# Hybrid trunk layer on one core: order of the first loads, small tables on the scalar engine's queue, first group's matmuls interleaved with the transposes of x

## The reference

```python
for l in range(DEPTH):                                  # DEPTH = 1, x is 1 x 256 x 2048 float32
    h = rmsnorm(x, pre_norm_g[l])
    proj = jnp.einsum('bsd,dn->bsn', h, w_in[l])        # 2048 x 18776
    (da_q, da_k, da_v, da_z, ml_qk, ml_v, ml_if, ml_o, ml_z,
     dsa_q, dsa_kv, idx_q, idx_k, idx_w, dsa_z, gates) = jnp.split(proj, split_points, axis=-1)
    y_a = diff_attention(...) * silu(da_z)
    y_b = mlstm(...) * silu(ml_z)
    y_c = dsa_attention(...) * silu(dsa_z)
    g = sigmoid(gates)
    mixed = sum over the three branches of g_b * (y_b @ w_branch[l, b])
    x = x + rmsnorm(mixed @ w_out[l], post_norm_g[l])
```

## Time and profile before

| | us |
|---|---|
| median of three runs | 1133.67 |
| span of the profiled execution, first to last instruction | 1131.5 |
| PE busy | 1110.0 (98%) |
| DVE busy | 657.7 (58%) |
| ACT busy | 549.5 (49%) |
| weights and x read from HBM | 202.57 MB, 181 GB/s over the span |

### The profile page before, as it was taken

The page is one execution under the profiler, slowest core; times in us unless marked ns, Lnnn a source line. Parts: engine busy times, 40 slices in busy tenths (PEclk is TensorE's granted clock), DMA queues, the critical chain, the costliest instruction groups (busy, mean ns, idle before and its releaser), DMA issues.

```text
span 1131.5 us, 15625 instructions
## 1 busy us (share of the span) xinstructions
PE 1110.0 (98%) x5143; PEld 915.0 (81%) x5143; DVE 657.7 (58%) x910; ACT 549.5 (49%) x736; POOL 70.8 (6%) x122
## 2 busy tenths in 40 slices
PE   7999999999999999999999999999999999999995
PEld 6788888888878888888887778888888888888884
DVE  4744444666566676665766566665556645556454
ACT  6644444555454554544546444454444544445442
POOL 1000000100100011120210000000000000000001
PEclk9999999999999999999999999999999999999998
DMA  8666666566556546666556556655555476676551
GB/s 245 223 190 192 197 188 197 173 170 183 167 169 175 167 140 184 192 180 184 169 168 192 164 157 191 205 167 163 166 163 160 129 222 191 197 238 229 196 195 75
DMA packets 112399, 205.09 MB, mean 181 GB/s; under 512 B 11064, under 2 KB 15728, under 8 KB 111984
## 3 DMA queue, kind: packets, MB, share of 16 engines
q1 hardware_dynamic: 112368, 204.70, 60.1%
HBM read 202.57 MB, written 2.10 MB: 181 GB/s over the span
## 4 chain that ended last, share of the span: by engine, by line
PE 95%; SPq 2%; DVE 1%; ACT 1%; issue 0%; DMA 0%; DVEq 0%; ACTq 0%
PE stream L1233 30%; PE stream L1235 30%; PE stream L1234 29%; SPq L367 1%; PE mixer L1469 1%; DVE area L1216 1%; DVE wlo L822 0%; PE mixer L1496 0%; PE mixer L1485 0%; PE mixer L1328 0%; PE mixer L1303 0%; PE mixer L1404 0%; PE mixer L1462 0%; PE mixer L1429 0%; PE mixer L1314 0%
## 5 line engine op out<-in xcount | busy, mean ns | idle before, releaser
L822 DVE TENSOR_TENSOR wlo<-raw,whi 128x1024 fp32r<-128x1024 f32 (+1 forms) x378 | 460.9, 1222 | 430.5 <-ACT whi L559 428.5
L559 ACT ACTIVATE whi<-raw 128x1024 fp32r<-128x1024 f32 (+1 forms) x378 | 397.7, 1054 | 553.6 <-PE stream L1235 537.9
L1233 PE MATMUL stream<-whi,xhi 128*128 128x512 f32 (+1 forms) x1312 | 518.6, 395 | 2.8 <-DVE wlo L822 2.4
L1235 PE MATMUL stream<-whi,xlo 128*128 128x512 f32 (+1 forms) x1312 | 510.1, 389 | 0.0
L1234 PE MATMUL stream<-wlo,xhi 128*128 128x512 f32 (+1 forms) x1312 | 509.0, 388 | 0.0
L1233 PEld LDWEIGHTS stream<-whi,xhi 128*128 128x128 f32 x1312 | 246.8, 188 | 56.6 <-issue 5.8
L1235 PEld LDWEIGHTS stream<-whi,xlo 128*128 128x128 f32 x1312 | 246.6, 188 | 51.6
L1234 PEld LDWEIGHTS stream<-wlo,xhi 128*128 128x128 f32 x1312 | 247.1, 188 | 48.1
L1233 PE MATMUL stream<-whi,yhi 128*128 128x512 f32 x192 | 77.1, 401 | 0.0
L1235 PE MATMUL stream<-whi,ylo 128*128 128x512 f32 x192 | 75.0, 391 | 0.0
L1234 PE MATMUL stream<-wlo,yhi 128*128 128x512 f32 x192 | 74.8, 390 | 0.0
(11 more groups left out here) (244 smaller groups left out, 567.9 us busy)
## 6 DMA issues: line engine op xcount, KB each, us to landing
raw<-in_w_in SPq DMA_DIRECT2D x288, 512.0 KB, 3.7
raw<-in_w_branch SPq DMA_DIRECT2D x48, 512.0 KB, 4.5
raw<-in_w_out SPq DMA_DIRECT2D x32, 512.0 KB, 3.7
mixed<-in_x SPq DMA_DIRECT2D x4, 512.0 KB, 6.0
raw<-in_w_in SPq DMA_DIRECT2D x8, 256.0 KB, 3.9
area<-in_x SPq DMA_DIRECT2D x2, 1024.0 KB, 9.2
out<-area SPq DMA_DIRECT2D x8, 256.0 KB, 2.3
raw<-in_dsa_w_uv SPq DMA_DIRECT2D x4, 256.0 KB, 3.0
```

What stands on the lines that cost most here:

```text
L559: nc.scalar.activation(whi[:, slot, :, 0:width], raw[:, slot, :, 0:width], ACT.Copy).then_inc(whi_ready, 1)
L822: nc.vector.tensor_tensor(wlo[:, slot, :, 0:width], raw[:, slot, :, 0:width], whi[:, slot, :, 0:width].bitcast(F32), ALU.subtract).then_in ...
L1233: nc.tensor.matmul(to, left_hi[:, kt, tokens], high, start=first, stop=False)
L1235: last = nc.tensor.matmul(to, left_lo[:, kt, tokens], high, start=False, stop=final)
```

## The change

SP: the three DMAs into `rows` leave SP's queue and are issued by ACT as its first instructions. x1 follows x0 directly, and then the order is small unit 0, x2, small unit 1, x3, small unit 2, small units 3 to 7, and last the six constants. Before, the constants stood ahead of unit 4. The loads of group PA follow as before, now behind the constants.

PE: after banks 0 to 3 of x it multiplies unit 0, transposes banks 4 and 5, multiplies unit 1, transposes banks 6 and 7, and then multiplies units 2 to 7.

ACT and DVE: the early units are handled one at a time, unit 0 after bank 1, unit 1 after bank 3, unit 2 after bank 5, unit 3 after bank 7. ACT's `square_x(1)` moves from behind the rounding of unit 7 to behind that of unit 5, and the rounding and the split of A0 move ahead of the square root and of the reciprocal.

```diff
@@ -97,7 +97,7 @@
                     turns, units, groups)
 
 
-EARLY_UNITS = {5: (0,), 7: (1, 2, 3)}
+EARLY_UNITS = {1: (0,), 3: (1,), 5: (2,), 7: (3,)}
 PS = Part(0, 0, 1, FULL_UNITS, 1)
 PA = PS.next(4, 2 * FULL_UNITS, 2)
 PB = PA.next(4, 2 * FULL_UNITS, 2)
@@ -371,21 +371,14 @@
             for n in range(X_LOADS):
                 part_of_x = slice(n * D_MODEL // X_LOADS, (n + 1) * D_MODEL // X_LOADS)
                 sp.dma_start(x_sb[:, :, part_of_x], x_d[:, :, part_of_x]).then_inc(x_landed[n], 16)
-                if n == 0:
-                    sp.dma_start(rows[40:56, :], pre_norm_g[0].rearrange("(b d) -> b d", d=P)).then_inc(rows_landed, 16)
-                    sp.dma_start(rows[0:32, :], ml_conv_w[0].rearrange("j (b d) -> (j b) d", d=P)
-                                 ).then_inc(rows_landed, 16)
-                    sp.dma_start(rows[32:40, :], ml_conv_b[0].rearrange("(b d) -> b d", d=P)).then_inc(rows_landed, 16)
-                if n >= 2:
-                    load_small(n - 2)
-            load_small(2)
-            load_small(3)
+                if n >= 1:
+                    load_small(n - 1)
+            for u in range(X_LOADS - 1, FULL_UNITS):
+                load_small(u)
             for to, of in ((lam_in[:, :, :].rearrange("p a b -> p (a b)"), da_lambda[0].rearrange("a b -> (a b)")),
                            (da_g[:, :], da_norm_g[0]), (ml_g[:, :], ml_norm_g[0]), (kv_g[:, :], dsa_kv_norm_g[0]),
                            (ik_g[:, :], dsa_ik_norm_g[0]), (gate_b[:, :], ml_gate_b[0].rearrange("a b -> (a b)"))):
                 sp.dma_start(to, of.partition_broadcast(P)).then_inc(consts_landed, 16)
-            for u in range(RING, FULL_UNITS):
-                load_small(u)
 
             with sp.Fori(0, PA.turns) as i:
                 for g in range(2):
@@ -566,6 +559,9 @@
                     nc.scalar.activation(to[t], stream[bank_pair][t][:, 0:width], ACT.Copy, scale=rstdx[:, t:t + 1]
                                          ).then_inc(banks_free, 1)
 
+            act.dma_start(rows[40:56, :], pre_norm_g[0].rearrange("(b d) -> b d", d=P)).then_inc(rows_landed, 16)
+            act.dma_start(rows[0:32, :], ml_conv_w[0].rearrange("j (b d) -> (j b) d", d=P)).then_inc(rows_landed, 16)
+            act.dma_start(rows[32:40, :], ml_conv_b[0].rearrange("(b d) -> b d", d=P)).then_inc(rows_landed, 16)
             act.wait_ge(cols_turned, 1)
             nc.scalar.activation(cols[:, :], M[0][:, 0:56], ACT.Copy).then_inc(cols_ready, 1)
             act.wait_ge(cols_ready, 1)
@@ -582,13 +578,14 @@
 
 
             square_x(0)
-            for u in range(FULL_UNITS // 2):
+            for u in range(FULL_UNITS // 2 + 1):
                 round_unit(PS, 0, u)
-            square_x(1)
+                if u == 1:
+                    square_x(1)
             act.wait_ge(msx_ready, 1)
             nc.scalar.activation(rstdx, rstdx, ACT.Sqrt).then_inc(stdx_ready, 1)
 
-            for u in range(FULL_UNITS // 2, FULL_UNITS):
+            for u in range(FULL_UNITS // 2 + 1, FULL_UNITS):
                 round_unit(PS, 0, u)
             act.wait_ge(rstdx_ready, 2)
             take_group(PS, 0, FULL_UNITS, 0, [small[:, t, :] for t in range(TILES)], SMALL)
@@ -849,12 +846,13 @@
                 split_unit(PS, 0, u)
             dve.wait_ge(ssx_ready, 2)
             nc.vector.tensor_scalar(rstdx, ssx, 1.0 / D_MODEL, EPS, ALU.mult, ALU.add).then_inc(msx_ready, 1)
+            split_unit(PS, 0, FULL_UNITS // 2)
             dve.wait_ge(stdx_ready, 1)
             nc.vector.reciprocal(rstdx, rstdx).then_inc(rstdx_ready, 1)
             dve.wait_ge(rstdx_ready, 1)
             nc.vector.tensor_scalar(half_rstdx, rstdx, 0.5, None, ALU.mult).then_inc(rstdx_ready, 1)
 
-            for u in range(FULL_UNITS // 2, FULL_UNITS):
+            for u in range(FULL_UNITS // 2 + 1, FULL_UNITS):
                 split_unit(PS, 0, u)
 
             dve.wait_ge(consts_landed, 6 * 16)
@@ -1256,11 +1254,14 @@
                                                    x_sb[:, t, kt * P:(kt + 1) * P], ident[:, :])
                 last.then_inc(x_turned, 1)
 
-            for b in range(8):
+            for b in range(4):
                 turn_x(b)
 
             pe.wait_ge(xlo_ready, 4)
             for u in range(FULL_UNITS):
+                if u in (1, 2):
+                    turn_x(2 * u + 2)
+                    turn_x(2 * u + 3)
                 pe.wait_ge(xlo_ready, UNIT_KT * (u + 1))
                 multiply(PS, 0, u, u, FULL_UNITS, 0, xhi, xlo, SMALL)
```

## The result

The changed kernel takes 1138.09 us in the median of four runs (1136.27 to 1139.65), the kernel before 1133.27 us in the same session (1132.83 to 1134.2). The ratio is 1.0044, with a 95% interval of 1.0032 to 1.0055: slower by 3.6 to 6.2 us, where the forecast was +3.2 us.

The account below looks back on a forecast made before the run. PE bounds the kernel, so only A4's start counts, set by `take_group`: 21.0 + 1.52 + 2.88 + 4.6 + 1.04 + 1.41 + 3.0 + 0.97 = 36.4 against 33.17, +3.2 us, 1136.9 us; range 1133.5 to 1138.8.

Parts of the forecast that it names:

- x's start: PE's start on x: set by x0 landing at 5.8 us (4.9 to 6.5), with the tables there by about 4.9.
- Interleaving: PE's early units and banks: 1.9 us a unit, 1.97 per two banks; ACT done with unit 3 at 20.0 us.
- SP's queue: SP from unit 3's split at 21.0 us: three issues 1.52, six constants 2.88; A0's load issued at 25.4.
- Flight of A0: A0's load from issue to landing: 4.6 us, bounds 3.7 and 5.7; it lands at 30.0 us.
- Three roundings and take_group: ACT behind the root: 3.0 us for three roundings, 0.97 for `take_group`, which ends at 36.4 us.
- take_group to A4: Small steps on DVE and ACT from `take_group`'s end to A4 on PE: unchanged 9.80 us, A4 at 46.2.
- rival 1: ACT never waits for A0, whose load gets out or lands in time: +0.2 us, 1133.9 us; chance 0.12.
- rival 2: PE is the bound up to A4, never waiting: A4 starts at 40.2, -2.8 us, 1130.9 us; chance 0.05.
- Rival 4: x3 lands late and holds PE's transposes: 1 us beyond the hidden part gives 1137.9 us; chance 0.02.
- Rival 3: PE's clock falls in the longer stall before A4, which runs at half speed: another 2.8 us, 1139.7; chance 0.04.

Follow-up runs that it names:

- e1: The changed kernel with SP issuing the six constants ahead of small unit 4 again: 1133.75 us, ratio 1.0001.
- e7: The kernel before plus 17 transposes of the identity on PE ahead of x, result unread: 1133.81 us, ratio 1.0002.
- e5: The changed kernel with the six constants issued by POOL instead of SP, after the fourth split: 1136.43 us, ratio 1.0030.
- e10: The changed kernel with the constants ahead of small unit 4 and ACT's and DVE's old order behind unit 3: 1135.52 us, ratio 1.0011.
- e6: The changed kernel with the three table DMAs back on SP and 17 transposes of the identity on PE ahead of x: 1139.70 us, ratio 1.0061.
- e9: The kernel before with the change's loads, but constants ahead of small unit 4, and `square_x(1)` directly behind `square_x(0)`: 1132.26 us, ratio 0.9992.
- e2: The changed kernel with the three table DMAs back on SP behind x0: 1139.41 us, ratio 1.0050.
- e3: The kernel before with only the change's loads (SP's new order, tables on ACT); PE, ACT and DVE keep their order: 1136.36 us, ratio 1.0024.
- e8: The kernel before with interleaving, the new x and small-unit load order, tables on SP, constants on POOL behind bank 5, 17 added transposes: 1135.01 us, ratio 1.0020.
- e4: The kernel before with only the new order on PE, ACT and DVE; SP's order and the tables as before: 1136.91 us, ratio 1.0029.

## Why the prediction was right, and where its size was off

The sign, the place and the chain were right: A0's load went out behind the constants at 25.27 (forecast 25.4), ACT stood still in front of it with root and `take_group` queued behind, A4 started by `take_group`'s chain, and nothing changed from there on. Run e1 shows it by undoing that one thing. The measured 1138.09 us lies in the range, near its upper end. By the steps:

| step | forecast | measured |
|---|---|---|
| PE begins on x | 5.8 | 7.14 |
| unit 3 rounded (T3) | 20.0 | 19.4 |
| unit 3 split | 21.0 | 20.6 |
| A0's load issued | 25.4 | 25.27 |
| A0 at ACT | 30.0 | 30.96 |
| `take_group` ends | 36.4 | 38.06 |
| A4 starts on PE | 46.2 | 47.51 |

- **x's start.** x0 did not set it. It landed 4.3 us after its issue, at 5.1; the tables did, at 6.8. I had let them land "by about 4.9 us", from their flight on SP's queue, where only x0's load was ahead of them, while I charged the company in flight to x0. The step failed by 1.3 us.
- **Interleaving.** That error was more than made good by a second one. I timed the transposes at 1.97 us for two banks from the earlier trace rows, twice. Behind unit 0 they took about 0.8 us, as the next matmul follows 0.79 us after them (13.89 to 14.68). The old figure was that of a PE at 1.2 GHz: run e7 turns the same banks in 1.1 us once PE has worked before them. T3 came out 0.6 us early, by luck: two errors of opposite sign.
- **SP's queue.** From unit 3's split to A0's issue were 4.67 us instead of 4.40. With the split 0.4 us early, the issue at 25.27 looks more exact than the working was.
- **Flight of A0.** This is the mis-sized term: 5.7 us, my upper bound, where I took 4.6. The row I took was of a load that went out when its slot came free, with the next 1.2 us behind it. Here four loads went out within 2 us, behind 0.5 MB of constants. Run e5 puts 6.95 us on the same load with the constants beside it and e1 3.6 us without, as does e10 with the loads crowded. I had this cost as a bound and not as a cause.
- **Three roundings and take_group.** The forecast was 3.0 us from A1 to `take_group`, without waits; it took 3.55, since A1 to A3 flew 7.6 to 8.9 us and ACT waited for two of them. A0's rounding, the table load and the root took 2.58 instead of 2.45.
- **take_group to A4.** 9.45 instead of 9.80 us. The time outside the profiled span was 1.8 us (1136.27 less 1134.5), where 2.2 was added.

The rivals: rival 1 (ACT never waits) and rival 2 (PE as the bound) fell, with a wait of 4.98 us and an A4 4.5 us later. Rival 4 fell as well: PE did not wait for x2 or x3. Rival 3 was half right. I gave it 0.04 with the argument that PE had idled 5.4 us at the start and still ran at 1.00. The clock did fall, not at A4 but within A0, in front of which PE had waited 2.38 us:

```profile
32.00:34.00 2.00, 0.67 (x2) 0.53 (x3) 1.56 (x3) 1.96 (x4) 0.00 (x0) 0.94 0.88 336
34.00:36.00 2.00, 2.00 (x6) 1.61 (x5) 1.30 (x2) 1.66 (x2) 0.00 (x0) 0.50 0.75 219
36.00:38.00 2.00, 2.00 (x7) 1.54 (x7) 1.93 (x2) 1.87 (x3) 0.00 (x0) 0.71 0.64 156
```

Matmuls of 512 columns came every 0.43 us there. It cost nothing by itself: A0 to A3 ended later, and PE's wait before A4 was 1.38 us instead of the 2.7 forecast. The argument was wrong at its root, see below. The Trainium skill's rule, "TensorE: Matmul & The Clock Gate", section "Why this matters for your kernels", that an idle gap between bursts brings 1.2 GHz back, agrees in kind with this stretch; I had set it aside on the strength of a column that could not speak against it. But not every such gap did: in e5 and e6 PE waited 2.56 us before A4, and the windows behind show 1.00. The row of e5:

```profile
46.12 0.50 PE L1232 MATMUL stream<-whi,xhi 128*128 128x512 f32 x1 [2.56 <-DVE wlo L820]
```

What stays open: whether e9's 0.08% is real, and how much of the spread of the changed kernel is the clock of its start. The mean granted clock of its four executions (0.995, 0.993, 0.995 and 0.993 for spans of 1134.5, 1137.9, 1136.4 and 1136.2 us) does not put them in order.

## What to carry to other kernels

When DMAs are moved in a queue that also waits for slots, look for the first big load behind their new place and ask two things: when it is issued, and what flies beside it; small broadcast loads cost more in the second way (2.5 us in run e5) than in the first (1.4). An order that interleaves compute with loads moves the time at which each load is wanted, so it must be costed with the load order, not by itself: each half alone and both together were slower here, by 2.8, 4.4 and 4.5 us. And where a start-up phase hides behind another engine's queue, making it faster gives nothing until that queue is shorter (17 added transposes: ratio 1.0002).

## What the runs showed of the hardware

- The granted clock in the windows read 1.00 from time zero in the kernel before, yet eight transposes took 1.97 us at 5.6 us and 1.03 us in the changed kernel at 13.9. In e2 unit 0's matmuls came every 0.29 us where they come every 0.16 at full rate, with the column again at 1.00. In e6, where PE had been busy earlier, the column shows 0.50 for the same matmuls. So in these traces the column says nothing about the stretch ahead of its first change; the spacing of matmuls does.
- In seven profiles the granted clock fell to 1.2 GHz in or soon behind a wait of PE of 1.97 to 2.61 us (2.38 before A0 in the changed kernel, 2.61 in e2 and 2.10 in e3 at the same place, 1.98 and 1.97 before unit 0 in e6 and e8, 2.04 and 1.97 before A4 in e1 and e10; e1's windows from 44 to 48 us show 0.51 and 0.64). Three waits as long passed without a fall (2.36 and 2.56 us in e6, 2.56 in e5), and in e7 and e9 it fell behind shorter ones (1.49 and then 0.48 us; 1.51 us). In the kernel before, e2, e4 and e7 it fell between 406 and 412 us with no wait of PE at all, in the other eight profiles it did not. So the length of the wait alone does not tell whether the clock falls. Where PE is the bound such a stretch costs it some 1.6 us, eight matmuls at 0.43 instead of 0.23 us.
- An issue took 0.43 to 0.63 us on ACT's queue (the tables), 0.43 to 0.47 on SP's for the constants in the changed kernel, and 0.53 to 0.72 us from POOL (e5).
